# A two-block transformer kernel: the projections' source moved 32 bytes, the activations that are loaded as weights moved by buffer

## What is computed

```python
def swiglu(x, w_gu, w_down):
    g, u = jnp.split(x @ w_gu, 2, axis=-1)
    return (jax.nn.silu(g) * u) @ w_down
# block 1, for each of 2 layers (D_FF = 2816)
x = layer_norm(DN_ALPHA * x + 0.5 * swiglu(x, ffn_w_gu[layer, 0], ffn_w_down[layer, 0]), ...)
...   # latent or sparse attention, memory attention, w_out, layer_norm
x = layer_norm(DN_ALPHA * x + 0.5 * swiglu(x, ffn_w_gu[layer, 1], ffn_w_down[layer, 1]), ...)
# block 2, for each of 2 layers: a recurrent mixer, then the experts
def peer_ffn(h, w_q, sub_keys, u_tab, v_tab):      # 16384 experts, 8 heads, top 16
    q = (h @ w_q).reshape(B, S, PEER_HEADS, 2, PEER_DQ // 2)
    scores = jnp.einsum('bshpd,hpkd->bshpk', q, sub_keys)
    ...                                             # ids and gates g of the 16 best
    act = jax.nn.gelu(jnp.einsum('thkd,td->thk', u_tab[idx], hx))
    return jnp.einsum('thk,thkd->td', g * act, v_tab[idx])
```

## Time and profile before

| | us |
|---|---|
| median of 3 runs | 3137.87 |
| lowest, highest | 3136.33, 3141.48 |
| span of the profiled execution | 3135.3 |
| TensorE matmuls busy in it | 3041.4 (97%) |
| VectorE busy | 2258.6 (72%) |
| ScalarE busy | 1475.7 (47%) |
| chain that ended last, share of TensorE | 92% |

### The profile page before, as it was taken

The page is one execution under the profiler, slowest core; times in us unless marked ns, Lnnn a source line. Parts: engine busy times, 40 slices in busy tenths (PEclk is TensorE's granted clock), DMA queues, the critical chain, the costliest instruction groups (busy, mean ns, idle before and its releaser), DMA issues.

```text
span 3135.3 us, 54521 instructions
## 1 busy us (share of the span) xinstructions
PE 3041.4 (97%) x19822; PEld 2758.6 (88%) x19822; DVE 2258.6 (72%) x4163; ACT 1475.7 (47%) x2483; POOL 114.9 (4%) x132
## 2 busy tenths in 40 slices
PE   8998999999999998899999999999999999999998
PEld 8986898998589987799999988887799999988887
DVE  7756777676565688689889955555579989975555
ACT  4425443433454465444544445553645544445554
POOL 0010111001010000000000000000100000000000
PEclk9999999999999999999999999999999999999999
DMA  8762686876135552145544455555335544455554
GB/s 322 279 262 86 251 294 236 289 280 224 59 124 186 174 171 98 54 162 182 181 142 140 141 181 192 191 193 196 126 135 181 181 155 141 139 170 194 193 191 152
DMA packets 124981, 567.91 MB, mean 181 GB/s; under 512 B 13872, under 2 KB 14000, under 8 KB 97328
## 3 DMA queue, kind: packets, MB, share of 16 engines
q1 hardware_dynamic: 108864, 504.41, 46.9%
q0 software_dynamic: 15264, 58.73, 5.4%
q10 hardware_dynamic: 720, 3.00, 0.2%
HBM read 565.03 MB, written 1.05 MB: 181 GB/s over the span
## 4 chain that ended last, share of the span: by engine, by line
PE 92%; DVE 5%; ACT 2%; issue 1%; DMA 0%; DVEq 0%; ACTq 0%
PE turn L353 51%; PE gather L353 40%; ACT arena L1361 1%; PE turn L868 0%; DVE arena L2599 0%; ACT hT L1361 0%; ACT L1361 0%; DVE ring_low L2147 0%; DVE arena L2458 0%; PE gather L662 0%; DVE arena L2290 0%; DVE ring_low L2140 0%; DVE arena L2285 0%; DVE arena L2054 0%; DVE arena L2407 0%
## 5 line engine op out<-in xcount | busy, mean ns | idle before, releaser
L1361 ACT ACTIVATE dense<-ring 128x1024 fp32r<-128x1024 f32 x544 | 575.8, 1059 | 388.4 <-PE gather L353 347.8
L2621 DVE TENSOR_TENSOR ring_low<-ring,dense 128x1024 fp32r<-128x1024 f32 x544 | 662.2, 1218 | 79.6 <-ACT dense L1361 77.7
L353 PE MATMUL turn<-expert_src_high,ring_low 128*128 128x256 f32 x2496 | 707.8, 284 | 0.0
L353 PE MATMUL turn<-expert_src_high,dense 128*128 128x256 f32 x2304 | 665.9, 289 | 1.2 <-DVE expert_src_low L2131 1.2
L353 PE MATMUL turn<-expert_src_low,dense 128*128 128x256 f32 x2304 | 653.5, 284 | 0.0
L353 PE MATMUL gather<-dense 128*128 128x512 f32 x2048 | 631.3, 389 | 2.1 <-DVE ring_low L2621 2.1
L353 PE MATMUL turn<-rounded 128*128 128x256 f32 x2816 | 514.1, 285 | 13.6 <-DVE ring_low L2147 11.8
L353 PEld LDWEIGHTS turn<-expert_src_high,ring_low 128*128 128x128 f32 x2496 | 479.7, 192 | 0.0
L353 PEld LDWEIGHTS turn<-rounded 128*128 128x128 f32 x2816 | 446.1, 194 | 16.8 <-DVE ring_low L2147 11.8
L353 PEld LDWEIGHTS gather<-dense 128*128 128x128 f32 x2048 | 384.5, 188 | 82.5 <-DVE ring_low L2621 2.9
L353 PEld LDWEIGHTS turn<-expert_src_high,dense 128*128 128x128 f32 x2304 | 443.5, 192 | 1.8 <-issue 1.8
(11 more groups left out here) (255 smaller groups left out, 3730.1 us busy)
## 6 DMA issues: line engine op xcount, KB each, us to landing
ring<-tiles_in SPq DMA_DIRECT2D x544, 512.0 KB, 3.3
ring<-stream SPq DMA_DIRECT2D x205, 1024.0 KB, 5.9
arena<-ada_in POOLq DMA_DIRECT2D x96, 512.0 KB, 4.5
arena<-tables_in POOLq DMA_DIRECT2D x6, 1024.0 KB, 7.3
arena<-keys_in SPq DMA_DIRECT2D x2, 1024.0 KB, 7.8
arena<-c_in POOLq DMA_DIRECT2D x3, 512.0 KB, 6.6
hT<-x_in SPq DMA_DIRECT2D x1, 1024.0 KB, 4.9
x_rows<-rows_in ACTq DMA_DIRECT2D x1, 1024.0 KB, 20.2
```

Of the source, the lines that this page charges most:

```text
L353: return nc.tensor.matmul(out, lhsT, rhs, start=start, stop=stop, skip_group_check=True)
L1361: return nc.scalar.activation(out, in_, func, **kw)
L2621: V.tensor_tensor(tile_words(t, ring_low).bitcast(R32), tile_words(t), tile_high[:, t % AHEAD, :], ALU.subtract).then_inc(S("tile_low"), 1)
```

## The change

No instruction is added, removed or moved: on all five engines the rows of the program stand in the same order with the same shapes and waits. Only addresses move. In words (addresses modulo 128 bytes, where not said otherwise):

- `hT` / `expert_src_low`, `gated`, `hidden` / `expert_src_high` move up by 32 bytes (`apart`), and a filler behind them makes `params` begin at a multiple of 128 again. So the source of the expert stages' projections is at 32 past a multiple of 128, its weights still at a multiple. The mixers' and output projections' use of these names, and `hT` as a source elsewhere, move too.
- The source of the feed-forward stages is at 32 bytes in stages 0 and 1, and one and two lines of 128 bytes further up in stages 2 and 3, which is at a multiple of 128 as before.
- The four homes of `hid_high` and of `hid_low` are at 64, 32, 16 and 0 bytes.
- The four homes of `expert_high` and of `expert_low` are at 64, 32, 256 and 128 bytes, of which the last two are multiples of 128.
- The weights stay where they were.

```diff
+LINE = 32
+APART = 8
+SOURCE_APART = (8, 8, 32, 64)
+HIDDEN_APART = (16, 8, 4, 0)
+EXPERT_APART = (16, 8, 64, 32)
...
         x_rows = sb("x_rows", [P, TT, DM])
+        sb("apart", [P, APART])
         hT = sb("hT", [P, KC, T])
...
+        sb("apart_end", [P, LINE - APART])
         params = sb("params", [P, N_PARAMS])
...
-        n_parts = 4 * HALF + 2 * KC * T + 8 * T
+        n_parts = 4 * HALF + 2 * KC * T + 8 * T + 10 * LINE
...
         w_high = parts.take(4, HALF)
-        hid_high = parts.take(4, T)
-        hid_low = parts.take(4, T)
-        src_high = parts.take(KC, T)
-        src_low = parts.take(KC, T)
-
-
-        n_dense = AHEAD * HALF + 8 * T
+        hid_high, hid_low = ([parts.take(T + LINE)[:, s:s + T] for s in HIDDEN_APART] for _ in range(2))
+        src_at, _ = parts.at, parts.take(2 * KC * T + 2 * LINE)
+
+        def source_parts(m):
+
+            words = Place(src_at + SOURCE_APART[m], n_parts, rounded)
+            return words.take(KC, T), words.take(KC, T)
+
+
+        n_dense = AHEAD * HALF + 8 * (T + 2 * LINE)
...
-        expert_high = dense.take(4, T)
-        expert_low = dense.take(4, T)
+        expert_high, expert_low = ([dense.take(T + 2 * LINE)[:, s:s + T] for s in EXPERT_APART] for _ in range(2))
         ring_words = ring[:, :, :].rearrange("p s w -> p (s w)")
-        rows = Place(gate_rows_at, SLOTS * PIECE, ring_words)
+        rows = Place(gate_rows_at + 16 * LINE, SLOTS * PIECE, ring_words)
...
+                src_high, src_low = source_parts(m)
...
-                    hid = (hid_high if high else hid_low)[:, (n + j) % 4, tt * P:(tt + 1) * P].bitcast(R32)
+                    hid = (hid_high if high else hid_low)[(n + j) % 4][:, tt * P:(tt + 1) * P].bitcast(R32)
...
-                    hid = (expert_high if high else expert_low)[:, n % 4, tt * P:(tt + 1) * P].bitcast(R32)
+                    hid = (expert_high if high else expert_low)[n % 4][:, tt * P:(tt + 1) * P].bitcast(R32)
```

More of the change, by code:

```diff
@@ L1435, in last_norm, with source_high @@
                     .then_inc(S("output_ready_s"), 1)
-            def source_high(norm, src_high=src_high):
+            def source_high(norm, src_high):
                 def chunk(k):
@@ L1617, in shared @@
                         .then_inc(S("cmp_hidden"), 1)
-                source = source_high(2)
+                source = source_high(2, source_parts(2)[0])
                 for k in range(KC):
@@ L1863, in hidden_high @@
                 def hidden_high(n, turns=0):
-                    run(expert_high[:, n % 4, :].bitcast(R32), slots[:, n + 12 * turns, :], ACT.Copy)\
+                    run(expert_high[n % 4].bitcast(R32), slots[:, n + 12 * turns, :], ACT.Copy)\
                         .then_inc(S("expert_high"), 1)
@@ L1918, in _ @@
             act.wait_ge(S("x_loaded"), 16)
-            first_source = source_high(None)
+            first_source = source_high(None, source_parts(0)[0])
             for k in range(KC):
@@ L1927, in _ @@
             first_weights(1)
-            layer_norm(1, source_high(1))
+            layer_norm(1, source_high(1, source_parts(1)[0]))
             ffn(1)
@@ L1936, in _ @@
             first_weights(3)
-            layer_norm(4, source_high(4))
+            layer_norm(4, source_high(4, source_parts(3)[0]))
             ffn(3)
@@ L2125, in output, with source_low @@
                                        final_row[:, half(b)], ALU.mult, ALU.mult).then_inc(S("output_ready"), 1)
-            def source_low(stage, src_high=src_high, src_low=src_low):
+            def source_low(stage, src_high, src_low):
                 def chunk(k):
@@ L2157, in hidden_parts @@
                 dve.wait_ge(S(full), n + 1)
-                V.tensor_copy(hid_high[:, n4, :].bitcast(R32), hidden[:, n4, :]).then_inc(S(high), 1)
+                V.tensor_copy(hid_high[n4].bitcast(R32), hidden[:, n4, :]).then_inc(S(high), 1)
                 dve.wait_ge(S(high), n + 1)
-                V.tensor_tensor(hid_low[:, n4, :].bitcast(R32), hidden[:, n4, :], hid_high[:, n4, :],
+                V.tensor_tensor(hid_low[n4].bitcast(R32), hidden[:, n4, :], hid_high[n4],
                                 ALU.subtract).then_inc(S(ready), 1)
@@ L2755, in hidden_low @@
                     dve.wait_ge(S("expert_high"), e0 + n + 1 + 12 * turns)
-                    V.tensor_tensor(expert_low[:, n % 4, :].bitcast(R32), slots[:, n + 12 * turns, :],
-                                    expert_high[:, n % 4, :], ALU.subtract).then_inc(S("expert_hidden"), 1)
+                    V.tensor_tensor(expert_low[n % 4].bitcast(R32), slots[:, n + 12 * turns, :],
+                                    expert_high[n % 4], ALU.subtract).then_inc(S("expert_hidden"), 1)
                 def down(n, turns=0):
@@ L2798, in chunks @@
                     chunk(k)
-            chunks(source_low(0))
+            chunks(source_low(0, *source_parts(0)))
             first_weights(0)
@@ L2807, in _ @@
             first_weights(1)
-            layer_norm(1, out_ends("out0", 0), source_low(1))
+            layer_norm(1, out_ends("out0", 0), source_low(1, *source_parts(1)))
             ffn(1)
@@ L2812, in _ @@
             first_weights(2)
-            chunks(source_low(2))
+            chunks(source_low(2, *source_parts(2)))
             ffn(2)
@@ L2819, in _ @@
             first_weights(3)
-            layer_norm(4, out_ends("out1", 1), source_low(3))
+            layer_norm(4, out_ends("out1", 1), source_low(3, *source_parts(3)))
             ffn(3)
```

## The result

| | before | changed |
|---|---|---|
| median of 20 runs, us | 3137.80 | 3132.76 |
| lowest, highest, us | 3136.32, 3155.42 | 3126.26, 3139.38 |
| span of the profiled execution, us | 3135.3 | 3133.1 |

The account below looks back on a forecast made before the run. TensorE was taken as the bound, through its matmuls' pace: -45 us (projections) + 9 us (homes) = -36 on a span of 3135.3, 3099, with 2.6 for the median 3102 us; 8 times in 10 between 3050 and 3158.

Parts of the forecast that it names:

- The kernel's time is the count of matmuls times their pace: Whole kernel: TensorE, busy 97% of the span, sets the time, and the change can only act on the matmuls' pace.
- Source 32 bytes up, 5 ns each, 45 us: Projections of expert stages and half the feed-forward ones: 9024 matmuls gain 5 ns each, 45 us less.
- the `hin_high` triple: Three projections, two with weights 64 bytes off level, 353.7 ns together; one's length, 278 against 283, gave the 5 ns.
- Source 128 and 256 bytes up, nothing: Feed-forward stages 2 and 3: 2112 projections stay level, 0 taken, bounds 4 ns either way, 8 us.
- Homes at 64 bytes, +8.5 ns; the others nothing: Down projections: 1032 on homes at 64 bytes lose 8.5 ns each, 9 us more; other homes taken as 0.
- the slow rival: Down projections lose more than projections gain: 23 us more, 3161 us if projections return to 120 ns; chance 0.19.
- Return to 120 ns: Rival for the shifted projections: pace falls back to 120 ns, no change, 3138 us, 3132 to 3144 with homes; chance 0.17.
- The down projections lose more: The slow rival: homes at 16 and 32 bytes cost like 64; needs projections gaining under 1.9 ns each; chance 0.19.
- The whole hold-up gone: Rival: what holds the float32r matmuls up vanishes; faster, with the far half below 3050 us; chance 0.18.
- VectorE stays covered: Expert stretch from 1563 to 1812 us: VectorE, busy 228.0 of 249.0 us, stays just covered by TensorE's 241 or 236.
- Everything else, nothing: Mixer and output projections, ScalarE, VectorE and `hT` load: 0 taken; the first two could be 3 and 1.4 us.

Follow-up runs that it names:

- run 1: Changed kernel with all homes of the loaded activations back at level places, source offsets kept: 3112.96 us, ratio 0.9919 to the kernel before.
- run 2: Changed kernel with every source back at its old, level place, homes kept as changed: 3160.44 us, ratio 1.0068 to the kernel before.
- run 4: Layout of the kernel before, with everything from `ring` on moved up together by 32 bytes: 3139.41 us, ratio 1.0001.
- first sweep: Changed kernel with feed-forward sources at 16, 48, 64, 96 bytes, expert source at 64, all homes off level: 3140.50 us in one run.
- Run 11: Changed kernel with feed-forward sources at 368, 288, 112, 32 bytes and all homes at multiples of 256: 3100.91 us in one run.
- fourth sweep: Changed kernel with level homes, feed-forward sources at 176, 208, 240, 108 bytes, expert source at 48: 3122.69 us in one run.
- the fastest kernel: Changed kernel with source at 112 bytes in all feed-forward stages, 32 for experts and `hT`, homes level: 3096.52 us, ratio 0.9869.
- the first two sweeps: The first sweep, and the changed kernel with sources at 160, 192, 224, 112 bytes, experts' at 96, other homes: 3140.50 and 3145.62 us, one run each.

## Why the prediction was wrong, step by step

- **The kernel's time is the count of matmuls times their pace, and the distance of two streams sets the pace.** Right. Runs 1, 2 and 4 show it from both sides, and run 4 excludes the absolute address for a shift of 32 bytes. Weight loads run beside the matmuls all the while (88% and 97% of the span busy before, 87% and 97% in the changed kernel), and 256 columns take 113.7, 116.7 or 120.0 ns by where the other operand lies.
- **Source 32 bytes up, 5 ns each, 45 us.** Right in sign, too large in size: 28 us, some 3.1 ns for each of the 9024. The step that failed is the splitting of the `hin_high` triple. I took the length of one member of it, 278 against 283 ns, for what a constant distance would do, on the premise that length and step move by the same amount. In the changed kernel the mean length fell by 4 ns and the step by 3. The row that answered was the pace of the whole triple, 117.9 ns: the first sweep has the experts' source at exactly its 64 bytes, and 1488 of them take 175.26 us, 117.8 ns each (in the triple only two of three matmuls lie off, so that the two agree so closely may be luck). Its 2.1 ns would have given 19 us, and 32 bytes gave a little more.
- **Source 128 and 256 bytes up, nothing.** Right for 256 (11.51 us), half right for 128 (11.38 and 11.52 in turn, under 1 us in all), and right for 128 too once the homes are level (run 1).
- **Homes at 64 bytes, +8.5 ns; the others nothing.** This is the second step that failed, and most of the rest went here. 64 bytes cost 6.9 ns, and 32 and 128 bytes cost 6.7 and 6.3, where I had 0. In place of 9 us it was 21, and the slow rival had priced the homes at 23. The rows said it: every 512-column row off level was longer, and I used that for the rival and not for the sum.
- **What is level.** I took every multiple of 128 bytes for level. Run 11 shows 256. So only one expert home of four stayed good, and in the feed-forward stages none did: a home there is 1152 bytes long in the changed kernel, four and a half times 256, so the four lie at 64, 160, 16 and 128 bytes within the period, and the last, which I had called unchanged, is 128 off. The table above has all of them near 233.
- **Return to 120 ns.** After each gap the projections do fall back into a rhythm, as this rival said, but into another one. In the changed kernel's stretch of expert tiles every second tile of 24 takes 2.83 us and the others 2.80, where before it was 2.87 (chain of waits):

```profile
1607.24 2.80 PE turn L363 x24
...
1610.94 2.83 PE turn L363 x24
```

- **The down projections lose more.** Their price was nearly right (21 us against 23), its other half was not: this rival needed projections that gain under 1.9 ns, and they gained some 3.1. The result lies between it and the forecast.
- **The whole hold-up gone, and times below 3050.** No run shows a pace for either: the shortest steady one of the projections is 113.3 ns (fourth sweep), that of the down projections 226.7 ns, and the fastest kernel takes 3096.52 us.
- **VectorE stays covered.** Right: from 1563 to 1812 us it is busy for 230.46 of 249 us, and TensorE waits there for none of its instructions (busy time by stretch). I looked at the wrong stretch for the tightest place, though: in the first 100 us of the unbroken piece VectorE is busy for 91.5 us before and 93.9 in the changed kernel, and it is there that the fourth sweep ran into it.

```profile
1563.00:1812.00 249.00, 248.43 (x2133) 247.68 (x2132) 230.46 (x519) 113.14 (x268) 0.00 (x0) 1.00 0.43 142
```

- **Everything else, nothing.** Right within some 1 us, but for the clock. The mixer's projections with `hin_high` got longer, 284 ns in the median against 278 in the earlier trace rows; in run 1, where the clock read 1.00 there, the piece of 384 takes 45.67 us against 45.90 before, so others gave it back. Instructions of tile hin_high on TensorE (ns least, median, most):

```profile
L363 PE MATMUL turn<-expert_src_high,hin_high x96: 278/284/287, 1119.5 to 1181.6; 128*128 128x256 f32 x96
```

Put together: -36 + 17 (projections) + 12 (homes) + 5 (all other steps, 4.2 of it with the clock) = -2, where the span has -2.2.

## What to carry to other kernels

Where TensorE is the bound and a matmul costs more than its columns add (here 120.0 ns for 256 columns, where 256 more cost 226.7 - 120.0 = 106.7), look at the distance between the moving and the stationary operand, here within the period of 256 bytes of a partition that run 11 showed, one kind of matmul at a time: 256-column streams gained up to 6.6 ns from some offsets, none or nearly none from others, and 512-column streams gained from none and lost 3 to 7 ns from most. Measure it for each stage in place: at 112 bytes the feed-forward stages ran at 113.7 ns and the expert stages at 118.7. One kernel with a distance for each stage measures four at once, if all else in it stays level. Read a whole piece and not its start, and look whether the next engine keeps up: one wait of 0.3 us turned 113.3 ns into 117.8. And when a change moves two things, price the one that looks harmless by the nearest row, even when that row is only of the same shape, before taking zero.

## What I had not expected of the hardware

**Several rhythms for one distance.** At 192 bytes the pieces of 96 projections take 10.90 and 11.31 us in turn, 113.5 and 117.8 ns, with the same distance in both, after other homes. At 112 bytes the feed-forward stages stay at 113.7 ns and the expert stages at 118.7 to 120. At 48 bytes a wait of TensorE turns 113.3 ns into 117.8. What precedes a piece, and a wait within it, are seen to change the rhythm; how they do is open.

**Less hold-up at the low clock.** In the kernel before and in the changed kernel the projections that run at the low level of the granted clock, 0.50, step by 213 to 214 ns, at level distances too, where at 1.00 the level ones step by 120.0. In the kernel before the first expert stage begins at the low level: from 1329.50 to 1332.70 us 15 steps, 213.3 ns each (busy time by stretch with the clock, then the order of time):

```profile
1329.00:1333.00 4.00, 3.85 (x18) 3.88 (x19) 3.17 (x10) 4.00 (x12) 0.00 (x0) 0.50 0.18 74
```

```profile
1329.50 0.41 PE L353 MATMUL turn<-expert_src_low,dense 128*128 128x256 f32 x1
...
1332.70 0.41 PE L353 MATMUL turn<-expert_src_low,dense 128*128 128x256 f32 x1
```

At half the clock twice 120.0 would be 240 ns. Half of 213.3 is 106.7, which is also what 256 more columns cost at 1.00 (226.7 - 120.0). My estimate from these two is that 13.3 ns of the 120.0 are hold-up at level distance, and that at 0.50 there is next to none.

**The clock after a gap.** In the changed kernel's profiled execution three short stretches ran partly at the low level of TensorE's granted clock, 0.50, where the execution of before had 1.00. After the gaps behind the feed-forward stage 3, in which TensorE is busy for 5.79 and 3.67 us of some 17, the first projections of the mixer are still at 0.50, and steps between them are 0.21 us in place of 0.12 (busy time by stretch, the second last column group is clock, then DMA share and GB/s):

```profile
1095.00:1105.00 10.00, 5.79 (x25) 4.33 (x24) 9.08 (x18) 2.19 (x7) 0.00 (x0) 1.00 0.43 145
1105.00:1111.90 6.90, 3.67 (x16) 3.27 (x16) 4.62 (x13) 5.54 (x18) 0.00 (x0) 0.56 0.23 95
1111.90:1116.00 4.10, 4.06 (x19) 4.09 (x20) 3.21 (x10) 4.10 (x12) 0.00 (x0) 0.50 0.00 0
```

In the kernel before the clock was back when the mixer began:

```profile
1103.00:1109.00 6.00, 3.67 (x16) 3.27 (x16) 3.76 (x12) 4.71 (x14) 0.00 (x0) 0.61 0.11 46
1109.00:1113.00 4.00, 3.88 (x32) 3.92 (x33) 3.13 (x9) 4.00 (x12) 0.00 (x0) 1.00 0.00 0
```

The three pieces affected are the mixer's 384 projections (47.48 us against 45.90 before), 20 matmuls at 259.55 us (7.12 against 5.57) and 112 on `hT` at 526.55 us (25.54 against the 24.45 of the earlier trace rows): 4.2 us together. For the second of these the clock reads 0.79 where it had 1.00, and in all other kernels it takes 5.57 us as before. The other two are not so clearly free of the layout. The mixer's 384 take 47.3 to 47.7 us, with the low level at their start, in the four profiled kernels whose homes are off level (the changed one, run 2 and the first two sweeps), and 45.4 to 45.9 us in the nine with level homes; the 112 on `hT` take 25.5 to 26.1 us in the same four, and 24.45 in seven of the nine. One profile of each kernel can't settle whether the homes have a hand in when the clock comes back. Over the 20 runs of the changed kernel the mean granted clock goes from 0.992, with a span of 3124.6 us, to 0.988, with spans of 3133.9 to 3137.7: each thousandth of mean clock goes with 2 to 3 us. So most of the spread between runs of this kernel goes with the clock, and a change of 5 us is to be read from the paces of its pieces rather than from one time.
